# A hybrid attention layer step: the order of a step's six score chunks in the dilated attention of the prompt

## The reference, cut to what matters

```python
DILATED_BRANCHES = ((128, 1), (512, 4), (2048, 16))
s = jnp.einsum('gnqhd,gnkhd->gnhqk', qb, kk).astype(jnp.float32) * ATT_SCALE + bias[None, None]
p, lse = masked_softmax_stats(s, valid[None, :, None])
o = jnp.einsum('gnhqk,gnkhd->gnqhd', p.astype(v.dtype), vv)
...
w = jnp.exp(lse - jnp.max(lse, axis=0, keepdims=True))
w = w / jnp.sum(w, axis=0, keepdims=True)
o = jnp.sum(w[..., None] * jnp.stack(outs, 0).astype(jnp.float32), axis=0)
```

## Time and profile before

| | |
|---|---|
| median of 3 runs | 1979.49 us |
| the profiled execution | 1979.52 us |
| its span on the core | 1977.7 us |
| mean granted TensorE clock | 0.992 of full speed |
| TensorE, matmuls | 1891.5 us, 96% of the span |
| TensorE, weight loads | 1751.7 us, 89% |
| VectorE | 1043.5 us, 53% |
| ScalarE | 443.2 us, 22% |
| GpSimd | 507.5 us, 26% |

### The profile page before, as it was taken

How to read it: one execution, slowest core, us unless ns; L and a number is a source line. 1 busy time by engine, 2 the same in 40 slices (tenths; PEclk the granted TensorE clock), 3 DMA queues, 4 the chain that set the end, 5 groups by cost and what they waited for, 6 DMA issues and landing times.

```text
span 1977.7 us, 33152 instructions
## 1 busy us (share of the span) xinstructions
PE 1891.5 (96%) x13253; PEld 1751.7 (89%) x13253; DVE 1043.5 (53%) x2108; ACT 443.2 (22%) x902; POOL 507.5 (26%) x371
## 2 busy tenths in 40 slices
PE   6999989999999999999999999999999999999987
PEld 6999987667767899998659999999999999999987
DVE  6698716666676455312553554544544454454455
ACT  5000114555555422101430220000000000000005
POOL 2332222010100145442002223333333333333320
PEclk9999999999999999999999999999999999999998
DMA  4399967586766512225431142342342342211102
GB/s 154 131 311 326 338 214 224 183 248 216 215 189 210 187 54 65 75 76 174 146 107 35 46 164 85 128 169 85 127 170 85 130 176 106 106 42 42 42 21 91
DMA packets 220002, 281.36 MB, mean 142 GB/s; under 512 B 7521, under 2 KB 206569, under 8 KB 218153
## 3 DMA queue, kind: packets, MB, share of 16 engines
q1 hardware_dynamic: 219901, 279.94, 43.4%
HBM read 266.48 MB, written 113.89 MB: 192 GB/s over the span
## 4 chain that ended last, share of the span: by engine, by line
PE 79%; DVE 9%; ACT 3%; SPq 3%; issue 2%; DMA 2%; POOL 1%; DVEq 0%; POOLq 0%; ACTq 0%
PE bank L1543 26%; PE bank L1579 12%; PE bank L1310 8%; PE bank L1071 7%; PE bank L1327 4%; PE bank L1018 3%; PE bank L1189 2%; DVE sp L2165 2%; PE bank L1290 2%; DMA w_raw<-in_w_in_dram 2%; SPq L650 2%; ACT p_T L1700 2%; PE bank L1162 2%; PE bank L1172 1%; PE bank L1505 1%
## 5 line engine op out<-in xcount | busy, mean ns | idle before, releaser
L923 POOL CAST w_hi<-w_raw 128x1024 fp32r<-128x1024 f32 x98 | 103.5, 1057 | 964.1 <-issue 313.7
L1543 PE MATMUL bank<-g_lo,w_hi 128*128 128x362 f32 (+1 forms) x1008 | 333.2, 331 | 0.0
L1543 PE MATMUL bank<-g_hi,w_lo 128*128 128x362 f32 (+1 forms) x1008 | 333.1, 330 | 0.0
L1543 PE MATMUL bank<-g_hi,w_hi 128*128 128x362 f32 (+1 forms) x1008 | 330.5, 328 | 0.0
L925 POOL TENSOR_TENSOR w_lo<-w_raw,w_hi 128x1024 fp32r<-128x1024 f32 x98 | 265.6, 2711 | 7.8
L2573 DVE TENSOR_TENSOR xT<-bank,xT 128x362 f32<-128x362 f32 (+1 forms) x264 | 139.8, 534 | 115.3 <-PE bank L1579 115.3
L1579 PE MATMUL bank<-act_hi,w_hi 128*128 128x364 f32 (+1 forms) x528 | 175.9, 333 | 16.2 <-DVE xT L2573 10.2
L1543 PEld LDWEIGHTS bank<-g_hi,w_lo 128*128 128x128 f32 x1008 | 191.0, 189 | 0.0
L1543 PEld LDWEIGHTS bank<-g_hi,w_hi 128*128 128x128 f32 x1008 | 189.7, 188 | 0.3 <-POOL w_lo L925 0.3
L1543 PEld LDWEIGHTS bank<-g_lo,w_hi 128*128 128x128 f32 x1008 | 189.6, 188 | 0.0
L1579 PE MATMUL bank<-act_lo,w_hi 128*128 128x364 f32 (+1 forms) x528 | 173.9, 329 | 0.0
(11 more groups left out here) (294 smaller groups left out, 3759.9 us busy)
## 6 DMA issues: line engine op xcount, KB each, us to landing
out_sk_dram<-in_cache_win_k_dram SPq DMA_DIRECT2D x24, 2040.0 KB
out_sv_dram<-in_cache_win_v_dram SPq DMA_DIRECT2D x24, 2040.0 KB
kb<-in_cache_win_k_dram SPq DMA_DIRECT2D x48, 512.0 KB, 4.9
vn<-in_cache_win_v_dram SPq DMA_DIRECT2D x22, 1024.0 KB, 7.9
w_raw<-in_w_in_dram SPq DMA_DIRECT2D x22, 512.0 KB, 11.0
w_raw<-in_w_ffn_gate_dram SPq DMA_DIRECT2D x22, 512.0 KB, 3.8
w_raw<-in_w_ffn_up_dram SPq DMA_DIRECT2D x22, 512.0 KB, 3.8
w_raw<-in_w_ffn_down_dram SPq DMA_DIRECT2D x22, 512.0 KB, 3.7
```

Of the source, the lines that this page charges most:

```text
L923: pool.tensor_copy(w_hi[slot][:, :], w_raw[slot][:, :]).then_inc(w_hi_done, 1)
L1543: last = pe.matmul(out, w, r, start=start, stop=stop)
```

## The change

The list that `chunks(d)` returns is turned round: the first 512 keys of the long block come first (m = 0, 1), its other (4-a) x 128 keys second (m = 2, 3), and the short block's (a+1) x 128 keys last (m = 4, 5). The banks go by m as before, and so do the waits of `scores` on `sc_free`. VectorE writes the long block's `nmax` after chunks 2 and 3 and the short block's after 4 and 5. The exponentials, the reciprocals and GpSimd's spreading take the long block (s = 1) first. No instruction is added or removed, and none changes its shape.

```diff
         def chunks(d):
             a = d % 4
-            return [(h, 0, 0, (a + 1) * P, 0, a, h) for h in range(2)] \
-                + [(h, 1, (a + 1) * P, 512, 0, 7 - a, 2 + h) for h in range(2)] \
-                + [(h, 2, (a + 1) * P + 512, (4 - a) * P, 512, 7 - a, h) for h in range(2)]
+            return [(h, 1, (a + 1) * P, 512, 0, 7 - a, h) for h in range(2)] \
+                + [(h, 2, (a + 1) * P + 512, (4 - a) * P, 512, 7 - a, 2 + h) for h in range(2)] \
+                + [(h, 0, 0, (a + 1) * P, 0, a, h) for h in range(2)]
...
-                for s in range(2):
+                for s in (1, 0):
                     for h in range(2):
-                        pool.wait_ge(rr_done, 4 * d + 2 * s + h + 1)
+                        pool.wait_ge(rr_done, 4 * d + 2 * (1 - s) + h + 1)
...
                 for e in range(4):
-                    h, s = e % 2, e // 2
+                    h, s = e % 2, 1 - e // 2
...
-                    if m < 2:
+                    if m >= 4:
                         dve.wait_ge(sc_free, 6 * d + m + 1)
                         dve.tensor_scalar(nmax[:, h, 0:1], smax[:, h, 0:1], -1.0, None, ALU.mult).then_inc(nm_ready, 1)
-                    elif m >= 4:
+                    elif m >= 2:
...
-                    dve.wait_ge(ex_done, 4 * d + 2 * s + h + 1)
+                    dve.wait_ge(ex_done, 4 * d + 2 * (1 - s) + h + 1)
...
+                inverse_sums(d, 1)
                 inverse_sums(d, 0)
-                inverse_sums(d, 1)
```

## The result

The changed kernel took 1990.63 us (median of 5 runs, 1987.54 to 1991.32) against 1979.49 us (median of 5, 1977.41 to 1983.68). The ratio is 1.0048, 95% interval 1.0034 to 1.0063, so +9.5 us (6.7 to 12.5) where 8.9 were forecast; the two medians lie 11.1 us apart. The profiled execution took 1987.54 us. The forecast's sign, size and mechanism held.

A forecast was written before the change was run, and what follows sets the result against it. No engine is full and the order of waits decides: even steps hang on VectorE, odd on TensorE. Losses of 2.65, 2.1, 1.3, 2.7 and 0.1 make 8.9 us, so 1979.5 + 8.9 = 1988.4 us, range 1984.6 to 1991.5.

The forecast's parts named there:

- (1): VectorE's first chunk, 512 columns wide, is ready later: +0.53 us for a = 0, 0.29 a = 1, 0.22 a = 2, 0 a = 3.
- (2): TensorE's wait at chunks 4 and 5: chunk 5 loads at 2.52 us in all steps, from 1.38 to 2.71 before.
- (3): Chunk 5's new width, 0.21 us per 128 columns: odd steps' sample scores +0.42 us (a = 1) and +0.45 (a = 3).
- The cover in even steps: TensorE's later sample scores in even steps cost nothing, hidden in its 0.75 us wait for VectorE's key copies.
- (4): Long exponentials begin earlier, short ones end later; over 1 us of cover before the reciprocals, so nothing lost or gained.
- The sum: Over the stage's steps: 2.65 (a = 0), 2.1 (a = 1), 1.3 (a = 2), 2.7 (a = 3), plus 0.1, making 8.9 us.
- the 0.1 of the forecast: Estimated loss of steps 0 and 1, the stage's start, together: 0.1 us.
- its upper bound of 0.53: The most that step 0 would pay, like other a = 0 steps: 0.53 us.
- covered: Rival: waits are elastic and shorter waits elsewhere make up the later start; no change, 1979.5 us; chance 0.08.
- both add up: Rival: in even steps TensorE's delay comes on top of VectorE's, 5.6 us more, 1994.0 us; chance 0.08.
- Faster through the exponentials: Rival: something waits for the long exponentials, which begin 0.27 to 1.6 us earlier; 22 us gained, 1957.9 us; chance 0.05.
- the lower end of the prediction's range: 1984.6 us, if chunk 5's width cost nothing, taking off 6 x 0.64 = 3.8 us.

The follow-up runs named there:

- the kernel of even steps alone: Kernel before with the new chunk order only in even steps (a = 0 and 2), the old order in odd ones; ratio 1.0021.
- Width alone: Kernel before with the order short block, long block's other keys, its first 512 keys, so only chunk 5's width is new (512 everywhere); ratio 1.0021.
- first chunk alone: Kernel before with the long block's first 512 keys first, then short block, then other keys; chunk 5 as wide as before; ratio 1.0038.
- their order alone: Kernel before with matmuls and chunks in the old order; only exponentials, reciprocals and GpSimd's spreading take the long block first; ratio 0.9991.
- the narrow order: Kernel before with the chunk order set for each kind of step, narrowest pair first (a = 0 unchanged); ratio 0.9987.

## Why the prediction was right

(1) VectorE's later first chunk: right, and it alone makes the loss of even steps, as the kernel of even steps alone shows. One size was off: a = 0 pays 0.64 and not 0.53. The forecast took 1.16 us from a step with a = 3 and set it against 0.63 in one with a = 0; but a = 0 steps have the wait for the strips in front of the first chunk, 0.11 us before and after, so they go to 1.27, and the cycle of four steps grew by 1.74 us for 1.62. The rows had it: 0.63 for 128 columns and 1.16 for 512 differ by 0.53, where the width's own 3 x 0.21 is 0.63 to 0.64.

(2) and (3) Chunk 5: right to 0.02 us in odd steps. Its load at 2.52 (2.53 measured for a = 3), the sample scores at 3.14 and 3.57 (3.16, 3.58). With a = 0 both are 0.11 or 0.12 later than forecast (2.63, 3.05), by the second wait, and that is covered. Width alone and first chunk alone, each tried by itself, gave what the sum has for them. The cover in even steps held.

(4) The exponentials: right. That a later last one costs nothing is shown by their order alone; that an earlier long one gains nothing, by the steps with a = 3 of the changed kernel (below).

The sum: the regular steps gave 5 x 0.64 or a little more (3.3 us with the 0.70 of steps 8 and 16), 5 x 0.43 (2.15), 6 x 0.22 (1.3), and 2.5 for the six steps with a = 3, one of which (step 7, 15.69 before) gave only 0.28: 9.3 us for the 8.9 forecast. The stage in the first profile grew by 11.5; the other 2.2 are step 0 (0.97) and the longer pause of step 15 (1.27). That the forecast of 8.9 lies so near the +9.5 of the times is in part luck, since its regular steps were 0.5 us too low and the whole is known only to 3 us.

For step 0 the 0.1 of the forecast was too low, and its upper bound of 0.53 too: 0.97 in this profile, 0.65 in the other. There VectorE came straight from its copies at 1.07 us in the kernel before, and now stands 0.50 us for the matmul and begins at 1.64. But step 0 also hangs on the first keys, for which TensorE waits here (0.58 us in the kernel before):

```profile
329.46 1.77 PE L1129 MATMUL bank<-ident,kb 128*128 128x128 f32 x13 [1.17 <-DMA kb<-in_cache_win_k_dram]
```

Where this wait is under 0.8 us, step 0 takes 10.42 or 10.43 in the traces with 128 columns first (five of them) and 11.02 to 11.07 in those with 512 (three); with a wait of 1.79 us it took 11.44 even in the old order. So some 0.6 us of the 0.97 are the change's, and the rest goes with late keys.

Of the rivals, "covered" and "both add up" are both refuted by the kernel with a wide chunk 5: a = 2 keeps its length though TensorE comes 0.44 us later. "Faster through the exponentials" is refuted by the changed kernel itself: with a = 3 the first long exponential begins 2.97 us after the start for 4.55 (step 11), as much earlier as the rival had it, and the step is 0.45 us longer. The Trainium skill's rule to look to the most-contended engine (Trace Analysis, Identifying the Most-Contended Engine) would have said no change; the ratio of 1.0048 goes against it here, as TensorE did the same work in both kernels and was only made to wait. The skill (TensorE: Matmul & The Clock Gate, Part 3: Packing small matmuls) says that matmuls in different row groups start some 4 ns apart and run side by side; the trace agrees for the pairs issued without a wait (the two heads' first matmuls start 6 to 7 ns apart, and chunks 0 to 3 of a step with a = 3, 1280 columns in all, end 1.35 us after the start, where 0.21 for each 128 makes 2.1). Chunks 4 and 5 start 0.61 us apart and overlap only in part: from the start of chunk 4 the two of step 11 take 1.73 us, where chunks 0 and 1, as wide, take 1.13. Width costs 0.21 us for each 128 columns in a pair too, so a pair wholly side by side would not have made chunk 5's width free, as the lower end of the prediction's range has it.

## What to carry to other kernels

Where an engine works off a row of results from another, the first one sets when it begins: put the narrowest first, if the second engine bounds the step. Where the producer must wait for buffers in the same row, its own last piece should be narrow too, because that one is on its path alone. Before moving work so that a long operation starts early, look in the list of waits whether anything waits for it.

## What the runs showed that was not expected

A second wait on a semaphore that had long been reached, ahead of the instruction that waits for a matmul, costs VectorE 0.11 us (1.27 to 1.16 us when it was taken earlier), and about 0.07 where it was moved to. The 17th matmul of one `values` call is followed by a pause of 0.6 to 2.5 us with no releaser, at one place of the program in every trace of this study, with a different length in two executions of the same instructions; it ends 2.4 to 2.6 us after a 16 KB packet on the instruction queue starts. Three irregular steps (1, 7 and 15) gave back 4.1 us in the narrow order's profile, where its other steps had gained 4.0, and two of them had a stretch of 3.4 us at the 1.2 GHz level, which cost 1.7 us in step 1. So a change of this size is better judged by the lengths of its repeating steps than by one time.
